# Output projection of a gated multi-branch mixer: seven block products instead of eight

## The chip, the cores and the metric

One Trainium2 chip (trn2), one of its cores. The metric is the device time of one execution in microseconds. All data is float32. A float32 product is made of three TensorE matmuls on operands split into a high part (rounded to fp32r) and a low part (the rest): high x high, high x low, low x high.

## What is computed

One layer, 1024 tokens of 1024 channels. Four branches A, B, C, M come from one input projection; each is projected by its own matrix, weighted by a gate per channel, and summed; the sum goes through the output projection, is added to the scaled input and normalised.

```python
def reference(x, mem, w_in, ...):
    proj = x @ w_in[l]
    ...
    gates = jax.nn.sigmoid(g.reshape(bsz, seq, N_BRANCH, D_MODEL))
    merged = (gates[:, :, 0] * y_a + gates[:, :, 1] * y_b
              + gates[:, :, 2] * y_c + gates[:, :, 3] * y_m)
    out = merged @ w_out[l]
    x = _layer_norm(ALPHA * x + out, ln_g[l], ln_b[l])
```

## The kernel before, in words

The kernel is written engine by engine: each engine has one list of instructions that it works through in order, and waits on semaphores (`s_...`) that other engines raise. So whatever stands behind a waiting instruction in the same list waits too. SyncE (SP) issues all DMAs, also in order.

**Input projection, pairs.** `PAIRS` lists 30 pairs of 256 columns of w_in; pairs 12 to 27 are the gates ("g"). From pair 2 on a pair is one 2x2 block product by seven products (`ORDER` = 1, 5, 6, 2, 7, 3, 4) instead of eight. GpSimd makes the four block sums of the weights (`s_make`, L1595). ScalarE makes the high part (`w_hi_make`, L1130) and GpSimd the low part (`lo_make`, L1571) of each product's weights into a ring of `RING` = 5 slots; the high part of product j waits for product j-5. ScalarE copies products 1, 5, 6 out of PSUM (`copy`, L1138), VectorE sums results 2, 7, 3 (`result`, L1749). Beside it VectorE runs the causal convolution of branch A (`conv_op`, L1785, accumulator in PSUM). The gates go to memory (`gate_scratch`) in 1 MB stores of SP. In pair 24 (`AG0 - 4`) the mean of A's LayerNorm is made: `mean_hi` on ScalarE (L1188) waits on `s_zst`, then its low part on VectorE (L1931), then TensorE's `channel_sum` before the fifth product of the pair.

**Branch projections.** Then come attention and the tiles of P_A, P_B, P_C, P_M (`P_TILES`), each 128 output channels by two halves of 512 tokens: P_C's first two tiles, the eight of P_M (12 matmuls each), then C2 to C7 of P_C (24 each). For a tile s, ScalarE and GpSimd split its weights (`split_w`, L1220, L1624, in two pieces); TensorE makes both halves; VectorE evacuates each with the gate (`p_half`, L2243); GpSimd adds the tile to `merged` (`add_back`, L1700), for P_M VectorE does (L2248). The gate of tile s is loaded by SP (L631) only when tile s-2 has been added, as they share a home. TensorE has four banks here: a half waits until the half four before it was evacuated.

**Output projection.** w_out (1024 x 1024) is loaded in eight blocks of 128 rows at C2 and beside the last tiles (L652, L655). From tile C4 on ScalarE and VectorE split `merged` (L1543, L2256) and w_out (L1550, L2261). TensorE accumulates 16 results (8 tiles of 128 tokens, 2 halves of 512 channels), each over 8 blocks k by three parts: `out_step`, L1074, 384 matmuls, of which the first four results go k by k as `merged` becomes ready. VectorE adds the residual (L2320), makes statistics (L2324, L2327), ScalarE the deviation, and VectorE normalises (L2332, L2337). GpSimd has no part in it.

## Time and profile before

| | us |
|---|---|
| median of 3 runs (lowest, highest) | 1223.47 (1223.08, 1223.71) |
| the profiled execution | 1223.87 |
| its span, first to last instruction | 1222.1 |
| TensorE busy | 1203.0 |
| VectorE, GpSimd, ScalarE busy | 781.5, 693.5, 539.5 |

The span is what the trace covers; the rest of the execution's time, 1.8 us, lies around it. The granted TensorE clock is 0.999 of full speed over the span. In the rows below, PE is TensorE, PEld its weight load, DVE VectorE, ACT ScalarE, POOL GpSimd, SP SyncE. L numbers are lines of the kernel before. "[x <-Y]" at the end of a row says that the engine stood idle for x us ahead of it and what ended the wait. "x2" at the end means that the row merges two instructions, from the start of the first to the end of the last.

### The profile page before, as it was taken

To read this page: it belongs to the slowest core of one execution; us is meant where nothing else is said; L and a number is where in the kernel's file an instruction comes from. 1 tells how busy PE (TensorE), PEld (TensorE's weight loads), DVE (VectorE), ACT (ScalarE), POOL (GpSimd) and SP (SyncE) were. 2 spreads that over 40 slices of the span, in tenths; PEclk is the share of its full clock that TensorE was granted. 3 is DMA by queue.
4 is the path that set the end of the run, shared out by engine and by line. 5 is a ranking of instruction groups with operands and counts; after the bars stand their busy time and mean duration, and the time that the engine had idled before them with its cause. 6 is when DMAs were issued, how large, how long until landed. Compare 5 with 4: busy or idle time off the path is not lost.

```text
span 1222.1 us, 15758 instructions
## 1 busy us (share of the span) xinstructions
PE 1203.0 (98%) x5704; PEld 999.2 (82%) x5704; DVE 781.5 (64%) x1285; ACT 539.5 (44%) x992; POOL 693.5 (57%) x550
## 2 busy tenths in 40 slices
PE   7999999999999999999999999999999999999997
PEld 6888888888888888888888888888888888878886
DVE  4723765677566674438587665666666786876755
ACT  5433434344443443557354565656556444315000
POOL 5677887887777777777226444455533225547000
PEclk9999999999999999999999999999999999999999
DMA  8022131232323423234412111111002533376131
GB/s 278 1 69 69 35 104 35 69 138 101 106 105 103 138 104 104 104 105 148 162 53 56 32 53 52 35 53 46 24 18 92 191 111 116 105 260 241 66 130 69
DMA packets 91277, 118.61 MB, mean 97 GB/s; under 512 B 6072, under 2 KB 72632, under 8 KB 91200
## 3 DMA queue, kind: packets, MB, share of 16 engines
q1 hardware_dynamic: 91200, 117.60, 29.2%
q8 instruction: 46, 0.75, 0.3%
q14 instruction: 31, 0.25, 0.1%
HBM read 92.39 MB, written 25.20 MB: 96 GB/s over the span
## 4 chain that ended last, share of the span: by engine, by line
PE 86%; DVE 7%; ACT 3%; issue 2%; DMA 1%; POOL 1%; DVEq 0%; SPq 0%; ACTq 0%
PE pj L745 11%; PE pj L746 11%; PE pj L747 11%; PE pj L816 5%; PE pj L817 5%; PE pj L818 5%; PE pj L1074 4%; PE pt L746 3%; PE pt L747 3%; PE pt L745 3%; PE po L930 3%; PE pt L917 2%; PE po L1074 2%; PE pt L1074 2%; PE pj L833 2%
## 5 line engine op out<-in xcount | busy, mean ns | idle before, releaser
L1571 POOL TENSOR_TENSOR ring_lo<-w_pair,ring_hi 128x512 fp32r<-128x512 f32 x168 | 232.3, 1385 | 111.3 <-ACT ring_hi L1130 111.1
L1624 POOL TENSOR_TENSOR w_lo<-w_raw,w_hi 128x128 fp32r<-128x128 f32 (+1 forms) x104 | 111.2, 1088 | 161.6 <-ACT w_hi L1220 159.5
L1130 ACT ACTIVATE ring_hi<-w_pair 128x512 fp32r<-128x512 f32 x168 | 105.1, 628 | 160.6 <-PE pj L747 108.6
L1785 DVE SCALAR_TENSOR_TENSOR po<-glu,cwa,po 128x512 f32<-128x512 f32 x232 | 159.4, 747 | 20.6 <-ACT po L1181 20.6
L745 PE MATMUL pj<-t_hi,ring_hi 128*128 128x512 f32 x392 | 152.8, 390 | 0.3 <-DVE slot L1749 0.3
L746 PE MATMUL pj<-t_lo,ring_hi 128*128 128x512 f32 x392 | 152.5, 389 | 0.0
L747 PE MATMUL pj<-t_hi,ring_lo 128*128 128x512 f32 x392 | 152.5, 389 | 0.0
L816 PE MATMUL pj<-xT_hi,w_hi 128*128 128x512 f32 x320 | 126.5, 395 | 0.0
L817 PE MATMUL pj<-xT_lo,w_hi 128*128 128x512 f32 x320 | 125.4, 392 | 0.0
L818 PE MATMUL pj<-xT_hi,w_lo 128*128 128x512 f32 x320 | 125.0, 391 | 0.0
L1664 POOL TENSOR_SCALAR probs<-probs,rinv 128x128 f32<-128x128 f32 (+3 forms) x32 | 57.9, 1810 | 110.8 <-DVE rinv L2103 110.8
L1749 DVE TENSOR_TENSOR slot<-pj,copy_p 128x512 f32<-128x512 f32 x56 | 38.5, 688 | 85.6 <-PE pj L747 85.4
L745 PE MATMUL pj<-xT_hi,ring_hi 128*128 128x512 f32 x224 | 87.1, 389 | 0.0
L746 PE MATMUL pj<-xT_lo,ring_hi 128*128 128x512 f32 x224 | 87.1, 389 | 0.0
L747 PE MATMUL pj<-xT_hi,ring_lo 128*128 128x512 f32 x224 | 87.1, 389 | 0.0
L745 PEld LDWEIGHTS pj<-t_hi,ring_hi 128*128 128x128 f32 x392 | 73.6, 188 | 16.5 <-DVE slot L1749 1.3
L747 PEld LDWEIGHTS pj<-t_hi,ring_lo 128*128 128x128 f32 x392 | 73.6, 188 | 15.3
L746 PEld LDWEIGHTS pj<-t_lo,ring_hi 128*128 128x128 f32 x392 | 73.6, 188 | 15.1
L1595 POOL TENSOR_TENSOR w_pair<-w_pair 128x512 f32<-128x512 f32 x56 | 81.8, 1461 | 6.2
L2115 DVE TENSOR_TENSOR pT_lo<-pt,pT_hi 128x512 fp32r<-128x512 f32 (+2 forms) x96 | 50.4, 553 | 48.4 <-ACT pT_hi L1396 48.4
L1749 DVE TENSOR_TENSOR slot<-pt,copy_p 128x512 f32<-128x512 f32 x28 | 19.4, 692 | 96.6 <-PE pt L747 96.6
L1396 ACT ACTIVATE pT_hi<-pt 128x512 fp32r<-128x512 f32 (+2 forms) x96 | 43.7, 489 | 77.4 <-PE po L930 67.8
(344 smaller groups left out, 2952.1 us busy)
## 6 DMA issues: line engine op xcount, KB each, us to landing
w_pair<-in_w_in SPq DMA_DIRECT2D x28, 1024.0 KB, 5.2
gate_scratch<-slot SPq DMA_DIRECT2D x16, 1024.0 KB, 4.0
gate<-gate_scratch SPq DMA_DIRECT2D x32, 512.0 KB, 3.8
w_raw<-in_w_in SPq DMA_DIRECT2D x20, 512.0 KB, 3.9
z_scratch<-slot SPq DMA_DIRECT2D x8, 512.0 KB, 2.6
bias<-cum_scratch SPq DMA_DIRECT2D x8, 512.0 KB, 3.8
wout_raw<-in_w_out SPq DMA_DIRECT2D x8, 512.0 KB, 5.5
x_tok<-in_x SPq DMA_DIRECT2D x8, 512.0 KB, 4.3
```

Of the source, the lines that this page charges most:

```text
L745: nc.tensor.matmul(dst, w_h, hi, start=k == 0 and p in (1, 2, 5), stop=False, skip_group_check=True)
L746: nc.tensor.matmul(dst, w_h, lo, start=False, stop=False, skip_group_check=True)
L747: mm = nc.tensor.matmul(dst, w_l, hi, start=False, stop=k == KH - 1, skip_group_check=True)
L816: nc.tensor.matmul(pj[:, bank, :], w_hi[:, j % 2, k, :], hi, start=k == 0, stop=False)
L817: nc.tensor.matmul(pj[:, bank, :], w_hi[:, j % 2, k, :], lo, start=False, stop=False)
L818: mm = nc.tensor.matmul(pj[:, bank, :], w_lo[:, j % 2, k, :], hi, start=False, stop=k == nk - 1)
L1074: mm = nc.tensor.matmul(out_bank(n), m, o, start=k == 0 and part == 0, stop=k == KT - 1 and part == 2)
L1130: nc.scalar.activation(ring_hi[:, j % RING, :, :], w_src(u, p), ACT.Copy).then_inc(s_rhi, 1)
L1571: nc.gpsimd.tensor_tensor(ring_lo[:, j % RING, :, :], w_src(u, p), ring_hi[:, j % RING, :, :], ALU.subtract).then_inc(s_rlo, 1)
L1595: nc.gpsimd.tensor_tensor(dst, in0, in1, op).then_inc(s_sadd, 1)
L1624: nc.gpsimd.tensor_tensor(w_lo[:, j % 2, k, :], w_raw[:, j % 2, k, :], w_hi[:, j % 2, k, :], ALU.subtract).then_inc(s_wlo, 1)
L1785: nc.vector.scalar_tensor_tensor(out=acc if n < PAD_A else src, in0=src, scalar=cwa[:, ct, n:n + 1], in1=acc, op0=ALU.mult, op1=ALU.add).t ...
```

## The change

The output projection becomes 2x2 block products too: a unit `u` of four is 256 tokens; it has the blocks a11, a12 (tokens 0 to 127 of the unit, channels 0 to 511 and 512 to 1023), a21, a22 (tokens 128 to 255), and w_out has four blocks of 512 x 512. Seven products a unit, each of 4 k x 3 = 12 matmuls with 512 columns, in the order 1, 5, 6, 2, 7, 3, 4.

- The seven operands from w_out: three are blocks of w_out, four are differences. GpSimd makes these in pairs 13/14, 16/17, 19/20, 22/23 (`block_sum`, four instructions of 512 columns for each of four groups of rows) on rows that SP loads in the pair before, and SP stores them to memory (`out_sums_scratch`, four stores of 1 MB). `mean_hi` now waits for the last of these stores, since they share a home.
- The seven operands, 1 MB each, are loaded at P_M tile 5, at C2, C4, C6, C7 and after, and split: ScalarE `out_block_hi` (2048 columns at once), VectorE `out_block_lo` in four instructions of 512 columns, blocks 0 to 2 behind C3, C4, C5, blocks 3 to 6 behind the last tiles.
- The sums of `merged` blocks are made in place (`merged_sum`): for unit 0 three on VectorE and one on GpSimd, for the others four on GpSimd. High parts of each product's `merged` operand on ScalarE, low parts on GpSimd (`out_lo`), ring of five.
- ScalarE copies products 1, 5, 6 out of PSUM, VectorE adds them to the scaled residual (`with_copy`) and then adds the banks of results 2, 7, 3, 4.
- The last two tiles of P_C run half 0 of both first, then half 1 of both; VectorE adds them to `merged` instead of GpSimd. P_M's odd tiles are added by GpSimd instead of VectorE.
- At the start ScalarE issues the loads of the first weight rows and VectorE makes the first high part of x.

```diff
+    OU = NT // 2
+    OSEQ = [(u, p) for u in range(OU) for p in ORDER]
+    NOQ = len(OSEQ)
+    OSLOT = {up: j for j, up in enumerate(OSEQ)}
+    O_RING = 5
+    OUT_B = {1: 0, 5: 1, 6: 2, 2: 3, 7: 4, 3: 5, 4: 6}
+    LAST_C = S_END - 2
+    def half_no(s, h):
+        return 2 * s + h + 1 if s < LAST_C else 2 * LAST_C + 2 * h + s - LAST_C + 1
+    SUMS_AT = (13, 16, 19, 22)
...
-        if br in (BR_B, BR_C):
+        if br == BR_B or br == BR_C and s < LAST_C or br == BR_M and dt % 2:
             ADD_NO[s] = len(ADD_NO) + 1
-        if br == BR_M:
+        elif br == BR_M:
...
+    ob_at = ((112, 120), (152, 160), (16, 24), (0, 8), (168, 176), (184, 144), (104, 128))
...
+    ob_rows = at_("out_b_rows", [P, 2, D], F32, 48 * KB)
+    o_ring_at = (64, 68, 192, 72, 76)
...
+    o_cp = {p: at_(f"out_copy_p{p}", [P, HALF], F32, o * KB) for p, o in ((1, 80), (5, 82), (6, 84))}
+    o_s1 = at_("out_s1", [P, KH, P], F32, 204 * KB)
...
-                for u in range(2):
-                    sp.dma_start(w_pair[u][:, k, :], pair_src(u, k, k + 1, 0, 2 * P).rearrange("p k c -> p (k c)")
-                                 ).then_inc(s_x11[k], 16)
+                if k:
+                    for u in range(2):
+                        sp.dma_start(w_pair[u][:, k, :], first_w_rows(u, k)).then_inc(s_x11[k], 16)
...
+                if u + 1 in SUMS_AT:
+                    k = SUMS_AT.index(u + 1)
+                    if k == 0:
+                        sp.wait_ge(s_zst, 64)
+                    else:
+                        sp.wait_ge(s_ots, 16 * k)
+                    for n in range(2):
+                        sp.dma_start(ob_rows[:, n, :], w_out[(k + KH * n) * P:(k + KH * n + 1) * P, :]).then_inc(s_wor, 16)
+                if u - 1 in SUMS_AT:
+                    k = SUMS_AT.index(u - 1)
+                    sp.wait_ge(s_ot, 4 * k + 4)
+                    sp.dma_start(t_dram[k, :, :, :], ob_rows[:, :, :].rearrange("p a (b c) -> p (a b) c", b=2)
+                                 ).then_inc(s_ots, 16)
...
+            def load_out_block(n):
+                if n in (0, 3, 5):
+                    kh, nh = {0: (0, 0), 3: (1, 0), 5: (1, 1)}[n]
+                    src = w_out[kh * HALF:(kh + 1) * HALF, nh * HALF:(nh + 1) * HALF].rearrange("(k p) n -> p k n", p=P)
+                else:
+                    src = t_dram[:, :, {1: 0, 4: 1, 6: 2, 2: 3}[n], :].rearrange("k p n -> p k n")
+                sp.dma_start(ob_raw[n][:, :, :], src).then_inc(s_wo[n], 16)
...
+                if s == S_OF[BR_M, 5]:
                     sp.wait_ge(s_tlo, TB_PAIR * CT + 2 * NT)
                     sp.wait_ge(s_pv, PV_PAIR * CT + 2 * NT)
                     sp.wait_ge(s_zpre, CT + MP)
-                    for k in range(2):
-                        sp.dma_start(wout_raw[k][:, :], w_out[k * P:(k + 1) * P, :]).then_inc(s_wo[k], 16)
-                elif s in (S_END - 5, S_END - 4, S_END - 3, S_END - 2, S_END - 1, S_END):
-                    k = s - (S_END - 5) + 2
-                    sp.dma_start(wout_raw[k][:, :], w_out[k * P:(k + 1) * P, :]).then_inc(s_wo[k], 16)
-            sp.wait_ge(s_wlo, 2 * S_END)
+                    load_out_block(0)
+                if s == S_OF[BR_C, 2]:
+                    load_out_block(1)
+                if s == S_OF[BR_C, 4]:
+                    load_out_block(2)
+                if s == S_OF[BR_C, 6]:
+                    sp.wait_ge(s_addm, ADDM_NO[S_OF[BR_M, 4]])
+                    sp.wait_ge(s_add, ADD_NO[S_OF[BR_M, 5]])
+                    load_out_block(3)
+                if s == S_OF[BR_C, 7]:
+                    load_out_block(4)
+                if s == S_END:
+                    load_out_block(5)
+                if s == S_END + 1:
+                    sp.wait_ge(s_pj, 2 * S_OF[BR_M, DT - 1] + 2)
+                    load_out_block(6)
...
+        def out_bank(u, p):
+            return bank((4 + 3 * u + {1: 0, 6: 0, 7: 0, 4: 0, 2: 1, 5: 2, 3: 2}[p]) % 8)
+        def out_src(u, p):
+            if p == 5:
+                return o_s1[:, :, :]
+            k0, n = {1: (0, 0), 6: (0, 0), 2: (KH, 0), 3: (KH, 0), 7: (0, 1), 4: (KH, 1)}[p]
+            return merged[:, k0:k0 + KH, (2 * u + n) * P:(2 * u + n + 1) * P]
...
+        def merged_sum(eng, ops, u, n):
...
+                dst, in0, in1, op = s1, a21, a22, ALU.add
+            elif n == 3:
+                eng.wait_ge(s_osum, O_SUM_NO[u, 1])
+                dst, in0, in1, op = a21, a11, a21, ALU.subtract
+            elif n == 2:
+                eng.wait_ge(s_osum, O_SUM_NO[u, 3])
+                eng.wait_ge(s_orl, OSLOT[u, 1] + 1)
+                dst, in0, in1, op = a11, s1, a11, ALU.subtract
+            else:
+                eng.wait_ge(s_osum, O_SUM_NO[u, 2])
+                eng.wait_ge(s_orl, OSLOT[u, 2] + 1)
+                dst, in0, in1, op = a12, a12, a11, ALU.subtract
...
+            for h in range(2):
+                for s in range(LAST_C, S_END):
+                    pe.wait_ge(s_pjfree, 2 * s + h - 3)
+                    p_steps(s, h, 0, CT, 2 * ((s + 1) % 2) + h)
...
+            def out_product(j):
...
+                elif p == 7:
+                    pe.wait_ge(s_ocp, 3 * u + 3)
+                elif p == 3:
+                    pe.wait_ge(s_ocp, 3 * u + 2)
+                else:
+                    pe.wait_ge(s_yk, 4 * u + 2)
+                pe.wait_ge(s_orl, j + 1)
+                if u == 0:
+                    pe.wait_ge(s_obl, OUT_B[p] + 1)
+                dst = out_bank(u, p)
+                for k in range(KH):
+                    w_h, w_l = o_ring_hi[j % O_RING][:, k, :], o_ring_lo[j % O_RING][:, k, :]
+                    hi, lo = ob_hi[OUT_B[p]][:, k, :], ob_lo[OUT_B[p]][:, k, :]
+                    nc.tensor.matmul(dst, w_h, hi, start=k == 0 and p in (1, 2, 5), stop=False, skip_group_check=True)
+                    nc.tensor.matmul(dst, w_h, lo, start=False, stop=False, skip_group_check=True)
+                    mm = nc.tensor.matmul(dst, w_l, hi, start=False, stop=k == KH - 1, skip_group_check=True)
+                mm.then_inc(s_out_pj, 1)
...
-                act.wait_ge(s_zst, 64)
+                act.wait_ge(s_ots, 16 * KH)
...
+            for u in range(2):
+                act.dma_start(w_pair[u][:, 0, :], first_w_rows(u, 0)).then_inc(s_x11[0], 16)
...
+                nc.scalar.activation(ob_hi[n][:, :, :], ob_raw[n][:, :, :], ACT.Copy, scale=0.5).then_inc(s_obh, 1)
...
+                if S_END - 5 <= s:
+                    out_block_hi(s - (S_END - 5))
+            for j in range(O_RING):
+                out_ring_hi(j)
+            for u in range(OU):
+                for p in ORDER:
+                    if p in (1, 5, 6):
+                        out_copy(u, p)
+                    if u == 0 and p in (1, 5):
+                        out_block_hi(5 + p // 5)
+                    if u and p == 5:
+                        out_std(2 * u - 1)
+                    if OSLOT[u, p] + O_RING < NOQ:
+                        out_ring_hi(OSLOT[u, p] + O_RING)
+                    if p == 4:
+                        out_std(2 * u)
+            out_std(NT - 1)
...
+                if n == 0:
+                    pool.wait_ge(s_wor, 32 * (k + 1))
+                else:
+                    pool.wait_ge(s_ot, 4 * k + n)
+                dst, in0, in1 = ((b11, b12, b11), (b12, b22, b12), (b22, b22, b11), (b21, b21, b22))[n]
+                nc.gpsimd.tensor_tensor(dst, in0, in1, ALU.subtract).then_inc(s_ot, 1)
...
+                    if u in SUMS_AT and p in (3, 4):
+                        block_sum(SUMS_AT.index(u), p - 3)
+                    if u - 1 in SUMS_AT and p in (1, 6):
+                        block_sum(SUMS_AT.index(u - 1), 2 + p // 6)
...
+            def out_lo(j):
+                pool.wait_ge(s_orh, j + 1)
+                nc.gpsimd.tensor_tensor(o_ring_lo[j % O_RING][:, :, :], out_src(*OSEQ[j]), o_ring_hi[j % O_RING][:, :, :],
+                                        ALU.subtract).then_inc(s_orl, 1)
+            for u in range(OU):
+                for p in ORDER:
+                    if p == 1 and u:
+                        merged_sum(pool, nc.gpsimd, u, 1)
+                        merged_sum(pool, nc.gpsimd, u, 3)
+                    out_lo(OSLOT[u, p])
+                    if p == 1 and u:
+                        merged_sum(pool, nc.gpsimd, u, 2)
+                    if p == 2:
+                        merged_sum(pool, nc.gpsimd, u, 4)
...
+            dve.wait_ge(s_x11[0], 48)
+            nc.vector.tensor_copy(xT_hi[:, 0, 0, :], r11[:, 0, :]).then_inc(s_xbh, 1)
...
-                if br == BR_M:
+                if br == BR_M and dt % 2 == 0:
                     dve.wait_ge(s_pjfree, 2 * s + h + 1)
                     dve.wait_ge(s_add, ADD_NO[S_OF[BR_C if dt < 2 else BR_B, dt]])
                     nc.vector.tensor_tensor(merged[:, dt, hs(h)], merged[:, dt, hs(h)], gate, ALU.add).then_inc(s_addm, 1)
+                if s >= LAST_C:
+                    dve.wait_ge(s_pjfree, half_no(s, h))
+                    dve.wait_ge(*added(S_OF[BR_M, dt]))
+                    nc.vector.tensor_tensor(merged[:, dt, hs(h)], merged[:, dt, hs(h)], gate, ALU.add).then_inc(s_addc, 1)
...
+            def out_block_lo(n):
+                dve.wait_ge(s_obh, n + 1)
+                for k in range(KH):
+                    op = nc.vector.scalar_tensor_tensor(out=ob_lo[n][:, k, :], in0=ob_raw[n][:, k, :], scalar=0.5,
+                                                        in1=ob_hi[n][:, k, :], op0=ALU.mult, op1=ALU.subtract)
+                op.then_inc(s_obl, 1)
...
+            for s in range(S_P + IN_M, LAST_C):
                 for h in range(2):
                     p_half(s, h, 2 * ((s + 1) % 2) + h)
-                if s >= S_END - 4:
-                    merged_rest(s - (S_END - 4))
-                    wout_rest(s - (S_END - 4))
-            for k in range(4, KT):
-                wout_rest(k)
-                merged_rest(k)
-            for t in range(NT):
+                if s == S_OF[BR_C, 3]:
+                    out_block_lo(0)
+                if s == S_OF[BR_C, 4]:
+                    out_block_lo(1)
+                if s == S_OF[BR_C, 5]:
+                    out_block_lo(2)
+            for h in range(2):
+                for s in range(LAST_C, S_END):
+                    p_half(s, h, 2 * ((s + 1) % 2) + h)
+                if h == 0:
+                    for n in (1, 3, 2):
+                        merged_sum(dve, nc.vector, 0, n)
+            for n in range(3, 7):
+                out_block_lo(n)
...
+            for u in range(OU):
+                for p in (1, 5, 6):
+                    with_copy(u, p)
+                for p in (2, 7, 3):
+                    out_result(u, p)
+                out_mean(2 * u)
+                if u < OU - 1:
+                    out_norm(2 * u)
+                    out_result(u, 4)
+                    out_mean(2 * u + 1)
+                    out_norm(2 * u + 1)
+            out_norm(NT - 2)
+            out_result(OU - 1, 4)
+            out_mean(NT - 1)
+            out_norm(NT - 1)
```

## Rows read from the trace of the kernel before

**Rows 1.** The profile's page, part 1: busy time, share of the span, instructions

```profile
PE 1203.0 (98%) x5704; PEld 999.2 (82%) x5704; DVE 781.5 (64%) x1285; ACT 539.5 (44%) x992; POOL 693.5 (57%) x550
```

**Rows 2.** Busy us in P_M, P_C, output: PE, PEld, DVE, ACT, POOL; clock, DMA

```profile
1071.40:1094.60 23.20, 22.70 (x98) 17.36 (x96) 18.45 (x27) 4.31 (x16) 11.01 (x18) 1.00 0.76 257
1094.60:1127.30 32.70, 32.70 (x144) 27.06 (x145) 21.52 (x23) 16.79 (x24) 24.04 (x15) 1.00 0.72 255
1127.30:1214.60 87.30, 87.30 (x386) 71.97 (x384) 55.21 (x71) 5.71 (x11) 3.31 (x1) 1.00 0.28 97
```

**Rows 3.** Chain that ended last: start us, us, what

```profile
1149.32 21.76 PE pj L1074 x96
```

**Rows 4.** Timeline, end of P_C: start us, us, engine, line, operation, tiles

```profile
1103.95 2.39 POOL L1700 TENSOR_TENSOR merged<-merged,gate 128x1024 f32<-128x1024 f32 x1 [1.67 <-DVE gate L2243]
...
1128.76 1.21 DVE L2256 SCALAR_TENSOR_TENSOR merged_lo<-merged,merged_hi 128x1024 fp32r<-128x1024 f32 x1
1128.91 3.31 POOL L1700 TENSOR_TENSOR merged<-merged,gate 128x1024 f32<-128x1024 f32 x1 [2.36 <-DVE gate L2243]
1129.89 3.41 DVE L2261 TENSOR_TENSOR wout_lo<-wout_raw,wout_hi 128x1024 fp32r<-128x1024 f32 x1
...
1140.04 1.21 DVE L2261 TENSOR_TENSOR wout_lo<-wout_raw,wout_hi 128x1024 fp32r<-128x1024 f32 x1
```

**Rows 5.** Timeline of POOL and DVE in a pair, at 561 us

```profile
561.06 1.28 POOL L1571 TENSOR_TENSOR ring_lo<-w_pair,ring_hi 128x512 fp32r<-128x512 f32 x1
561.21 2.22 DVE L1956 TENSOR_TENSOR glu<-glu,slot 128x1024 f32<-128x1024 f32 x1
562.49 2.11 POOL L1595 TENSOR_TENSOR w_pair<-s_w,w_pair 128x512 f32<-128x512 f32 x1
```

**Rows 6.** Timeline of DVE and POOL in a gate pair, at 337 us

```profile
337.08 7.32 DVE L1785 SCALAR_TENSOR_TENSOR po<-glu,cwa,po 128x512 f32<-128x512 f32 x11
342.26 1.29 POOL L1571 TENSOR_TENSOR ring_lo<-w_pair,ring_hi 128x512 fp32r<-128x512 f32 x1 [1.91 <-ACT ring_hi L1130]
344.98 1.28 POOL L1571 TENSOR_TENSOR ring_lo<-w_pair,ring_hi 128x512 fp32r<-128x512 f32 x1 [1.43 <-ACT ring_hi L1130]
```

**Rows 7.** End of P_C: POOL, SP, DVE; the page's gate load

```profile
1120.81 5.75 POOL L1700 TENSOR_TENSOR merged<-merged,gate 128x1024 f32<-128x1024 f32 x2
1123.24 0.33 SPq L631 DMA_DIRECT2D gate<-gate_scratch  x1
gate<-gate_scratch SPq DMA_DIRECT2D x32, 512.0 KB, 3.8
1127.56 1.27 DVE L2243 SCALAR_TENSOR_TENSOR gate<-gate,pj 128x512 f32<-128x512 f32 x2
```

**Rows 8.** The mean in pair 24: us to landing of a store; ACT, DVE

```profile
gate_scratch<-slot SPq DMA_DIRECT2D x1, 1024.0 KB, 4.3
...
478.20 1.05 ACT L1188 ACTIVATE ln_mean_hi<-ln_sum 128x1024 fp32r<-128x1024 f32 x1
479.29 1.47 DVE L1931 TENSOR_TENSOR ln_mean_lo<-ln_sum,ln_mean_hi 128x1024 fp32r<-128x1024 f32 x1 [4.45 <-ACT ln_mean_hi L1188]
482.63 0.69 DVE L1749 TENSOR_TENSOR slot<-pj,copy_p 128x512 f32<-128x512 f32 x1 [1.87 <-PE pj L747]
```

**Rows 9.** Timeline of the start: ACT, SP's queue

```profile
0.71 1.28 ACT L1118 ACT_TABLE_LOAD   x1 [0.71 <-PEq L2365]
1.16 0.89 SPq L522 DMA_DIRECT2D w_pair<-in_w_in  x2
5.27 0.63 ACT L1118 ACTIVATE xT_hi<-r 128x512 fp32r<-128x512 f32 x1 [3.27 <-DMA w_pair<-in_w_in]
```

**Rows 10.** PE at the end of P_M

```profile
1094.58 0.50 PE L833 MATMUL pj<-z_hi,w_hi 128*128 128x512 f32 x1 [0.28 <-DVE gate L2243]
```

**Rows 11.** DVE in the tail

```profile
1216.08 0.21 DVE L2327 BATCH_NORM_AGGREGATE mv<-ostats 128x2 f32<-128x12 f32 x1
1216.73 1.27 DVE L2332 SCALAR_TENSOR_TENSOR y_tok<-y_tok,mv,lng_b 128x1024 f32<-128x1024 f32 x1
```

More of the change, by code:

```diff
@@ L670, in _ @@
+            for u in range(1, OU):
+                for q in range(2):
+                    t = 2 * u + q
+                    sp.wait_ge(s_yk, 4 * u - 1 + q)
+                    sp.dma_start(x_tok[:, q, :], x[t * P:(t + 1) * P, :]).then_inc(s_xtk[q], 16)
+                    store_tile(t - 2)
+            store_tile(NT - 2)
             for h in range(2):
@@ L1102, in w_src @@
+            for j in range(NOQ):
+                out_product(j)
         def w_src(u, p):
```

251 lines of the change are left out of this document (132 added, 119 removed).

## Prediction

> **What bounds the kernel now.** I read the table of busy times first: TensorE is busy 98% of the span [rows 1]. So work taken from TensorE is worth its full time, unless an engine that feeds it falls behind. Next I read the stretches that the change touches. From the first P_M tile to the end of P_C, TensorE has hardly a gap, and the output projection is a solid block of 87.3 us [rows 2]; the chain gives 96 of its matmuls 21.76 us, so 0.2267 us each [rows 3]. In the P_C stretch GpSimd is busy 24.0 of 32.7 us and VectorE 21.5; in the output stretch GpSimd does next to nothing (3.3 us) [rows 2]. The change fills exactly this empty engine, so the last view is how VectorE and GpSimd behave when both are busy.
>
> **That view decides the case.** A GpSimd add of 1024 columns takes 2.39 us alone; started at 1128.91, just after a VectorE instruction with two SBUF inputs, it takes 3.31. The VectorE subtraction of 1.21 us alone takes 3.41 when it meets that add [rows 4]. The times fit one pattern to a tenth: the one that comes second stands still until the first has ended (1129.9 + 2.3 = 1132.2 for GpSimd; VectorE then ends at 1133.3), and they take turns, one instruction each. The same at 561: VectorE comes 0.15 us after a GpSimd instruction and takes 2.22 instead of 1.1; the next GpSimd instruction takes 2.11 instead of 1.3 [rows 5]. A VectorE instruction with a PSUM input takes no part: eleven in 7.32 us (0.66 each) run beside a GpSimd instruction that keeps its 1.29 [rows 6]. I count 0.6 us for a 512-column VectorE instruction (two in 1.27 [rows 7]) and 1.25 for a 512-column one of GpSimd.
>
> The Trainium skill says this too (SBUF — State Buffer, "Who interferes with whom"): a VectorE instruction with two SBUF inputs and a GpSimd one that reads SBUF exclude each other for the whole instruction. By that rule the trace agrees, and it speaks against this change; by a shared-bandwidth view (both somewhat slower) the waits below would be about halved. No number here needs the page.
>
> **Part 1, products.** 8 tokens x 2 halves x 8 k x 3 = 384 matmuls become 28 products x 12 = 336. 48 x 0.2267 = **-10.9 us**. A product is 12 x 0.2267 = 2.72 us. The shapes are the same, so the price is.
>
> **Part 2, feeding the first seven products.** Let Z be the end of the last tile's first half (C7, h 0); two more halves follow, so product 1 is due at Z+5.4 and product 4, the last of the seven, at Z+5.4+6x2.72 = Z+21.8. Product 4 waits for VectorE's reading of product 7's bank (s_yk 2). VectorE has in its queue ahead of that:
> - C7 h 0, evacuation and add: 1.3
> - three merged sums, each waiting for the one before: 2.0
> - both second halves, evacuation and add: 2.7
> - the low parts of blocks 3 to 6, four pieces each, 16 x 0.6: 9.6
> - three residual adds: 1.8; result 2 with its statistics and result 7: 1.9
>
> Together 19.3 us. It can't start before the gate of C7 is there. Its load waits for GpSimd's add of C5: the first of two adds begun at 1120.81 ends at about 1123.2, the load is issued at 1123.24 [rows 7], the median from issue to landing is 3.8 [rows 7], and Z in this trace is 1127.3 - 5.4 = 1121.9: so Z+5.2. With no turns the result is there at Z+24.5, a stall of 2.7.
> With turns: 22 to 25 of those instructions have two SBUF inputs, all 16 pieces among them. GpSimd meanwhile has six low parts of the first unit (products 5, 6, 2, 7, 3, 4), its fourth sum, then three sums and three low parts of the second unit: 13 x 1.25 = 16.3. They all read SBUF and interleave one by one with the pieces; a piece costs 1.85 instead of 0.6. Z+24.5+16.3 = Z+40.8, a stall of 19.0 in all, spread over products 2, 7, 3 and 4 (a block takes 7.4 us where a product takes 2.7). From below: only the seven GpSimd instructions that product 4 itself needs (8.8), less 4.2 that fit under VectorE's seven PSUM instructions: stall 7.3. If C7's gate comes 2 us earlier, 17. I take **+18** (2.7 to 20), near the upper end, because rows 4 and 5 show turns each time that both engines are ready. From the second unit on VectorE has 12 us of work in 19 (three residual adds, four results with statistics at 1.2, two tiles' normalising at 2.7 from rows 11), and GpSimd 11 x 1.25 = 13.8 with a lead of five ring slots: no stall, at most 1.
>
> **Part 3, blocks 0 to 2 beside P_C.** Before, a tile's extra VectorE work was two instructions of 1024 columns, each at most one turn. Now it is four pieces after C3, C4, C5: 2.4 us, plus turns with GpSimd's two w_lo pieces (1.4) and its add (2.4 [rows 4]): 6.2, with two evacuations 7.4 per tile of 5.44. VectorE falls back 2 us a tile over three tiles; TensorE has four banks, half of that shows, and the add, the gate load and the next evacuation go later with it. **+3** (0 to 5). The block loads are the bytes of before in other pieces; the first comes earlier, into the P_M stretch, where the DMA engines are busy 76% [rows 2]: 0, up to +2 inside that range.
>
> **Part 4, P_M.** Odd tiles' adds go from VectorE (two of 0.6) to GpSimd (2.4, 11 us busy in 23 [rows 2]). TensorE loses 23.2 - 8 x 2.72 = 1.4 us here; the last wait, for VectorE, is at 1094.58 [rows 10]. The first part of the loss is a late gate, which stays. **-0.3** (-1.3 to +1).
>
> **Part 5, sums of w_out on GpSimd.** Sixteen of 1.3 us, four over two pairs. A pair has idle stretches of 1.91 and 1.43 before its low parts [rows 6], and these run some three products ahead of their use (a low part is released by the product five before it: 5 x 2.72 = 13.6, less 0.6 and 1.3, less the queue). The first sum waits for its rows, behind a gate store, until about 8 us into the pair; GpSimd and, behind it, the low part of product 4 wait, due at 16.3. VectorE's work there has PSUM inputs, no turns. Cost 0 (0 to +1). If the cover goes, each late sum costs 1.3.
>
> **Part 6, the new wait of the mean.** ScalarE's mean_hi now waits for the fourth sums store, issued behind the 1 MB gate store of 473.8. One such store lands after 4.3 us [rows 8], at 478.1; the second goes out 0.4 us behind it and lands between 478.5 (all beside the first) and 482.4 (all after it). I take the middle, 480.6. mean_hi ran at 478.20, so it comes 2.5 later, ends 3.5 after 478.2 at 481.7 and holds up the copy of product 6, which still comes in time; VectorE's low part (1.47) ends at 483.3, and TensorE wants it when product 2 ends, at 482.6 [rows 8]. **+0.9** (0 to +2.5).
>
> **Part 7, start.** The second weight issue goes from SyncE at 1.6 to ScalarE at 1.2, and VectorE makes the first xT_hi, so ScalarE starts on the weights 0.54 us sooner after 5.27 [rows 9]. -0.9 if both count; 0 if ScalarE's table load of 1.28 us stays ahead of the issues. TensorE is full from there on, so it counts. **-0.7**.
>
> **Part 8, tail.** In the last unit tile 6 is normalised before tile 7's last half is read. Result 3 is ready 2.72 before the end: statistics, mean 1.6, two instructions of 1.27 with the reciprocal: free at end+1.65 instead of at once. The deviation now runs beside the centring, -0.4 of the 0.65 between aggregate and centring [rows 11]. **+1.3** (0.8 to 2).
>
> **Sum.** -10.9 + 18 + 3 - 0.3 + 0 + 0.9 - 0.7 + 1.3 = +11.3. The profiled execution took 1223.87 (span 1222.1 and 1.8 around it), 0.4 above the median 1223.47; so 1234.8.
>
> **Rivals.**
> - *Pieces go in a bunch.* VectorE runs the four pieces of a block without letting GpSimd in, since no wait stands between them. For: no row shows four such instructions in a row. Against: at 1129.9 VectorE's next instruction was ready and GpSimd still got its turn [rows 4]. A block then costs 2.4 + 1.25: turns 6 to 8 instead of 13, stall 11 to 12, P_C +1: -10.9+11.5+1+1.2 = +2.8, and up to +6: 1226 to 1230. Slower still, but half.
> - *TensorE stays the bound* (other side, faster). GpSimd has its low parts done before VectorE comes to the blocks, so few turns fall in the stretch, and C7's gate comes at Z+3. The place is the wait of product 4 for s_yk 2; it decides when VectorE's queue with its turns ends before Z+21.8+10, a stall under 10. With stall 3 and P_C 0: -10.9+3+1.2 = -6.7, 1217; with no stall 1214. For: the lead of five slots, and TensorE's solid block in spite of such turns in P_C before. Against: 19.3 us of VectorE's own work from Z+5.2.
> - *The sums starve the ring in the gate pairs* or the mean's wait is long: up to +3 on top of any case.
> - The seven products don't come down to 336 matmuls: hardly, the loops say so.
>
> **Chances.** Turns one by one, my forecast: 0.52, own range 1230 to 1239. Bunched or half: 0.19, 1225 to 1230, with a tenth of it within 0.2%. TensorE bound: 0.27, 1213 to 1221. Rest 0.02. A measurement of this kernel can tell about 0.2% (2.4 us) from no change. Slower by more 0.68, within 0.06, faster 0.26. The range for 8 in 10 has to reach into both: 1215 to 1239.
>
> **What would show it.** In the profile after: 336 output matmuls of 0.227 pitch; TensorE idle before products 2, 7, 3 and 4 of unit 0, released by VectorE's out_b_lo; these pieces at 1.8 us, not 0.6, with GpSimd's out_ring_lo between; GpSimd instructions of 1.9 us there. Units 1 to 3 without gaps. If the pieces show 0.6 each, Part 2 is wrong; if TensorE's gaps in the output stretch sum to under 8 us, the forecast's sign is wrong. Wrong too would be a mean that waits for nothing, or a first matmul as late as before.

## The result, and the profile after

The kernel after takes 1239.29 us (median of 6 runs), the kernel before 1223.59 beside it: a ratio of 1.0125, 95% interval 1.0110 to 1.0139. I had forecast 1234.8, slower by turns of VectorE and GpSimd, range 1215 to 1239. The profiled execution of after took 1237.01 (span 1235.2), 13.1 us of span more than before; the account below is for that execution. The runs of this kernel lie on two levels, near 1237.2 and near 1241.2, and one run of 6877 us stands apart; without it the median is 1237.4. So the median of all six is 0.3 above the top of my range, and that of the five is inside it. What is known of the two levels is told with the experiments.

The page, part 1, of the kernel after (it answers to [rows 1]):

```profile
PE 1197.8 (97%) x5656; PEld 991.6 (80%) x5656; DVE 814.2 (66%) x1309; ACT 556.4 (45%) x1022; POOL 786.1 (64%) x609
```

The busy time of TensorE fell by only 5 us, not by 11, and GpSimd has 93 us more. Busy time in windows of after, for P_M, P_C, the output projection and ten microseconds inside it (columns as in [rows 2]):

```profile
1074.44:1100.83 26.39, 23.05 (x97) 17.53 (x96) 15.23 (x22) 4.30 (x16) 19.55 (x21) 1.00 0.80 256
1100.83:1133.88 33.05, 33.05 (x145) 26.96 (x146) 24.83 (x27) 13.31 (x16) 24.08 (x17) 1.00 0.87 299
1133.88:1226.55 92.67, 81.70 (x337) 65.07 (x335) 85.17 (x93) 28.94 (x49) 66.58 (x40) 0.94 0.27 95
1145.00:1155.00 10.00, 6.77 (x18) 5.04 (x19) 10.00 (x7) 4.28 (x6) 9.25 (x7) 0.66 0.00 0
```

Against [rows 2]: the products are 28 x 12 = 336 matmuls, as forecast (the window counts 337), but they take 92.7 us for 87.3; P_M, where I had forecast a small gain, takes 26.4 for 23.2; P_C, where I had forecast a loss of 3, takes 33.05 for 32.7. In the last row VectorE is busy all of the time, GpSimd nearly so, TensorE two thirds, and its granted clock is 0.66.

Where TensorE stood still in the output projection (timeline: start, us, the instruction; in brackets the idle time before it and what ended it):

```profile
1147.89 0.76 PE L1210 MATMUL pt<-out_b_hi,out_ring_hi 128*128 128x512 f32 x1 [4.35 <-DVE out_b_lo L2443]
1160.30 0.77 PE L1210 MATMUL po<-out_b_hi,out_ring_hi 128*128 128x512 f32 x1 [3.76 <-DVE out_b_lo L2443]
1166.34 0.50 PE L1210 MATMUL pt<-out_b_hi,out_ring_hi 128*128 128x512 f32 x1 [1.70 <-DVE y_tok L2524]
```

These are products 2, 3 and 4 of the first unit; with two small ones (0.72 and 0.34) the gaps sum to 10.9 us. Behind product 4 there is none. The two engines that feed it, VectorE's 16 pieces in one row and three of GpSimd's instructions beside them:

```profile
1140.93 21.64 DVE L2443 SCALAR_TENSOR_TENSOR out_b_lo<-out_b_raw,out_b_hi 128x512 fp32r<-128x512 f32 x16
1149.45 1.73 POOL L799 TENSOR_TENSOR out_s<-merged 128x512 f32<-128x512 f32 x1
1151.25 1.61 POOL L799 TENSOR_TENSOR merged<-merged 128x512 f32<-128x512 f32 x1
1157.90 1.71 POOL L1875 TENSOR_TENSOR out_ring_lo<-merged,out_ring_hi 128x512 fp32r<-128x512 f32 x1
```

**The account.** TensorE's place, after less before: first matmul of L892 (L783 of the kernel before) 18.69 - 19.78 = -1.1; at the mean 485.63 - 482.43 = +3.2; first P_M matmul 1074.44 - 1071.39 = +3.05; first matmul of C2 1100.83 - 1094.58 = +6.25; first output matmul 1133.88 - 1127.39 = +6.5; last matmul's end 1226.49 - 1214.60 = +11.9; end of span +13.1. So the start gave 1.1, the pairs and the mean cost 4.3, P_M 3.2, P_C 0.2, the output 5.4, the tail 1.2 (mean to P_M -0.15).

### The profile page after: what moved, and what is told of

The parts are those of the page before. It is cut to its first block, busy times and chain, and to the rows that moved or that the text cites. A ratio compares the mean times of both kernels' runs of the same rounds, so it can differ in the third digit from the quotient of the medians.

```text
span 1235.2 us, 15869 instructions
## 1 busy us (share of the span) xinstructions
PE 1197.8 (97%) x5656; PEld 991.6 (80%) x5656; DVE 814.2 (66%) x1309; ACT 556.4 (45%) x1022; POOL 786.1 (64%) x609
## 4 chain that ended last, share of the span: by engine, by line
PE 78%; DVE 8%; DMA 4%; ACT 3%; issue 3%; POOL 3%; SPq 0%; DVEq 0%; ACTq 0%; POOLq 0%
PE pj L854 10%; PE pj L856 10%; PE pj L855 10%; PE pj L925 5%; PE pj L926 5%; PE pj L927 5%; PE pt L855 3%; PE pt L856 3%; PE pt L854 3%; PE po L1039 3%; PE pt L1026 3%; DMA gate<-gate_scratch 2%; DVE out_b_lo L2443 2%; PE pj L1009 1%; PE pj L1011 1%
## 5 line engine op out<-in xcount | busy, mean ns | idle before, releaser
L1965 DVE SCALAR_TENSOR_TENSOR po<-glu,cwa,po 128x512 f32<-128x512 f32 x232 | 159.5, 748 | 23.2 <-ACT po L1298 23.2
```

What stands on the lines that cost most here:

```text
L1965: nc.vector.scalar_tensor_tensor(out=acc if n < PAD_A else src, in0=src, scalar=cwa[:, ct, n:n + 1], in1=acc, op0=ALU.mult, op1=ALU.add).t ...
```

## Experiments

In the table each kernel's stretches are between matmuls of its own profile: the start of the mean's first matmul; from the first to the last P_M matmul (M); from there to the first output matmul (C); from there to the last (O). Times in us, medians of 4 or 5 runs (of 6 for after); the ratio is to the kernel before on the same chip.

| kernel | median | ratio, interval | mean at | M | C | O |
|---|---|---|---|---|---|---|
| before | 1223.6 | | 482.4 | 22.5 | 33.5 | 86.8 |
| after | 1239.3 | 1.0110 to 1.0139 | 485.6 | 25.1 | 34.4 | 92.2 |
| e1_whole | 1236.7 | 1.0097 to 1.0127 | 487.8 | 23.8 | 35.9 | 89.2 |
| e2_wait | 1234.9 | 1.0080 to 1.0112 | 485.4 | 25.3 | 34.4 | 88.3 |
| e3_filler | 1241.2 | 1.0121 to 1.0154 | 488.3 | 24.0 | 35.0 | 93.7 |
| e4_nosums | 1233.7 | 1.0069 to 1.0102 | 482.1 | 25.4 | 34.3 | 91.9 |
| e5_adds | 1239.9 | 1.0113 to 1.0162 | 488.3 | 25.3 | 34.9 | 95.0 |
| e6_load | 1240.5 | 1.0125 to 1.0156 | 488.0 | 23.9 | 37.6 | 92.2 |
| e7_shift | 1233.3 | 1.0065 to 1.0099 | 482.0 | 25.3 | 34.4 | 92.3 |
| e8_all | 1232.3 | 1.0059 to 1.0089 | 482.1 | 24.9 | 40.6 | 84.5 |
| e9_both | 1237.2 | 1.0097 to 1.0129 | 488.3 | 22.9 | 35.2 | 92.0 |
| e10_best | 1229.1 | 1.0038 to 1.0070 | 482.9 | 22.1 | 35.5 | 88.2 |
| e11_part | 1230.0 | 1.0041 to 1.0075 | 481.9 | 25.0 | 34.4 | 88.0 |
| e12_clock | 1229.4 | 1.0031 to 1.0059 | 482.6 | 23.0 | 34.6 | 89.6 |

The interval of after overlaps those of e1, e2 (barely), e3, e5, e6 and e9: by their time alone these are not told from it, and what they show is read from stretches of one profile each. The other six are faster than after. Where the output stretch is that of after, O is 91.9 to 92.3 in five kernels and 95.0 in e5, whose profile is of its slowest run (1243.7).

My theory for the output stretch was turns: a VectorE instruction with two SBUF inputs and a GpSimd instruction exclude each other and alternate. The rivals were a proportional slowdown and VectorE's own work.

**GpSimd held back (e2_wait).**

```diff
+                    if p == 1 and u == 1:
+                        pool.wait_ge(s_obl, 7)
                     if p == 1 and u:
                         merged_sum(pool, nc.gpsimd, u, 1)
```

> GpSimd waits until VectorE has made the low parts of all blocks before it starts on the sums of the second unit; nothing else is changed. Theory (turns): of the GpSimd instructions between 1140.9 and 1159.6 the last six belong to the second unit and are not needed before 1168. Without them the last ten pieces have no turn, VectorE ends them some 7 us sooner (1155 for 1162.5), and the kernel takes about 1230 to 1231. Product 1 of the second unit is then fed just in time (three GpSimd instructions, 3.9 us, after 1155). Rival (VectorE's own work sets the stall, not the turns): no gain, and up to 4 us of new waiting for GpSimd, 1237 to 1241.

Measured: 1234.9, less gained than either number of the theory, but its mechanism shows. VectorE's 16 pieces and what GpSimd did, in this kernel's timeline:

```profile
1140.84 15.15 DVE L2445 SCALAR_TENSOR_TENSOR out_b_lo<-out_b_raw,out_b_hi 128x512 fp32r<-128x512 f32 x16
1156.07 2.88 POOL L799 TENSOR_TENSOR out_s<-merged 128x512 f32<-128x512 f32 x1 [6.65 <-DVE out_b_lo L2445]
1159.76 0.50 PE L1210 MATMUL pt<-out_b_hi,out_ring_hi 128*128 128x512 f32 x1 [1.14 <-DVE y_tok L2526]
1181.60 0.50 PE L1210 MATMUL po<-out_b_hi,out_ring_hi 128*128 128x512 f32 x1 [2.35 <-DVE y_tok L2526]
```

The same pieces take 15.15 us for 21.64: six GpSimd instructions fewer beside them, 6.5 / 6 = 1.08 us for each turn. One by one, eleven pieces in after take 1.74 to 1.78 us and five 0.68; here five take 1.75 to 1.78 and eleven 0.68. Product 4 starts 25.6 us after the first output matmul for 32.5. So the turns are real and their work came too early: it belonged to the second unit. But 2.35 us come back in the second unit (last row): GpSimd, now late, meets VectorE's normalising there (four instructions of 1.9 to 2.2 us for 1.28 in after; the three residual adds take 5.2 in both kernels).

**Whole blocks (e1_whole).** One instruction of 2048 columns for the four pieces.

```diff
-                for k in range(KH):
-                    op = nc.vector.scalar_tensor_tensor(out=ob_lo[n][:, k, :], ...
+                nc.vector.scalar_tensor_tensor(out=ob_lo[n][:, :, :], ...
```

> The low part of each block of w_out is one VectorE instruction of 2048 columns instead of four of 512. Theory (each VectorE instruction with two SBUF inputs lets one GpSimd instruction go first): the 16 pieces of blocks 3 to 6 took 21.6 us, of which 16 x 0.6 to 0.68 is their own; as four instructions they have at most four or five turns of 1.3, so some 15 to 16 us; TensorE's stalls in the output stretch fall from 16.4 to about 10, and the time from 1237.2 to about 1231. Rival (the two engines slow each other in proportion to their bytes): the same 21 us, 1237. Second rival: GpSimd now stands still 2.4 us at a time, its own low parts come late and TensorE waits for these instead, 1234 to 1237.

Measured: 1236.7; O falls by 3.0, half of what I expected, and C grows by 1.5. From its timeline:

```profile
1142.63 13.23 DVE L2442 SCALAR_TENSOR_TENSOR out_b_lo<-out_b_raw,out_b_hi 128x2048 fp32r<-128x2048 f32 x4
1147.11 9.89 POOL L1875 TENSOR_TENSOR out_ring_lo<-merged,out_ring_hi 128x512 fp32r<-128x512 f32 x3
1155.79 5.14 DVE L2509 SCALAR_TENSOR_TENSOR x_tok<-x_tok,out_copy_p 128x512 f32<-128x512 f32 x3
```

The blocks take 13.2 for 21.6, which rules out a slowdown in proportion to bytes: the bytes are the same. But GpSimd now pays 3.3 us for each low part that takes 1.25 alone, and its turns of the second unit fall on the three residual adds, 5.1 us for 1.9. The turns were moved, not removed; the second rival of this run is half right. The Trainium skill (SBUF — State Buffer, "Who interferes with whom") has the lock held for the whole instruction; by that rule a long instruction hurts the other engine in proportion to its length, and this trace agrees (a low part of 1.25 us alone takes 3.3 beside 2048 columns, 1.7 beside 512).

**Does the clock cost anything? (e3_filler)**

```diff
                 if u == 0:
+                    for _ in range({2: 17, 3: 14}.get(p, 0)):
+                        nc.tensor.matmul(bank(7), ob_hi[1][:, 0, 0:P], ob_hi[1][:, 0, :], ...)
                     pe.wait_ge(s_obl, OUT_B[p] + 1)
```

> TensorE gets 17 matmuls of its own before the wait of product 2 of the first unit and 14 before that of product 3, into a bank that nobody reads: 3.85 and 3.2 us at 0.2267 each, inside the waits of 4.35 and 3.76 that the trace shows there. Nothing that others wait for comes later. Theory: the granted clock fell to 0.66 to 0.85 in this stretch because TensorE stood still, and that costs 5.5 of the 16.4 us lost; with the filler the clock stays at 1.0 and the time falls to 1232 to 1234. Rival: the clock falls there for another reason, or the slow matmuls only fill time in which VectorE is the bound anyway: 1237, with longer waits in place of the slow matmuls.

Measured: 1241.2, O 93.7: the rival. The clock of 1145 to 1155 was 1.00 instead of 0.66, and product 4 started 32.4 us after the first output matmul, as in after (32.5). Its start is set by VectorE, so slow matmuls ahead of it fill a wait and cost nothing. Drops came at other places: behind a wait of 2.7 us before product 7, and behind the wait of 2.6 us before product 4, where some ten matmuls ran at a pitch of 0.43; the latter nothing hides.

**The pairs (e4_nosums, e7_shift).** e4 leaves out every `block_sum`, and SyncE's store waits for the rows instead, so that blocks 1, 2, 4 and 6 hold plain rows. Of e7:

```diff
-                    if u in SUMS_AT and p in (3, 4):
-                        block_sum(SUMS_AT.index(u), p - 3)
-                    if u - 1 in SUMS_AT and p in (1, 6):
-                        block_sum(SUMS_AT.index(u - 1), 2 + p // 6)
+                    if u - 1 in SUMS_AT and p in (6, 7, 3, 4):
+                        block_sum(SUMS_AT.index(u - 1), (6, 7, 3, 4).index(p))
```

> GpSimd makes no block sums of w_out in the gates' pairs; the rows are loaded and stored as before, so blocks 1, 2, 4 and 6 are plain rows and the output is not the reference's. Theory (GpSimd stood 4.4 us for the rows, then ran behind; its late sums of w_pair held up ScalarE, which held up the convolution's first copy, behind which VectorE read a bank 2.5 us late): the 2.7 us lost before the mean go, the mean's own wait of 0.9 stays, 1234 to 1234.5. Rival a (the loads and stores of 6 MB disturb the pairs): 1237. Rival b (the late mean comes from the same backlog of GpSimd): 1233.

> The four block sums of a group of rows are made one pair later, in one pair, after the low parts of products 6, 7, 3 and 4, where GpSimd had idle stretches of 1.3, 1.9 and 1.4 us before the change, and the rows have long landed. Theory (standing 4.4 us for the rows and sums ahead of s_w is what set GpSimd back): the wait of 2.5 us at 414 goes and the time falls to 1233.5 to 1234.5; the last store goes out up to 4 us later, so the mean may wait 1 to 3 instead of 0.9, in which case 1235 to 1236. Rival (GpSimd has no room for 5.2 us in a pair of 19, wherever they stand): 1237 or more.

Measured: 1233.7 and 1233.3; the mean starts at 482.1 and 482.0 for 485.6. The loads and stores are there in both, so they are not the cause, and GpSimd has room for the sums, so that isn't either: it is where they stand (e7 takes away both GpSimd's standing for the rows and their places ahead of s_make; which of the two counts isn't told apart). Kernel after, timelines of GpSimd, ScalarE, VectorE, TensorE:

```profile
384.91 1.29 POOL L1755 TENSOR_TENSOR out_b_rows<-out_b_rows 128x512 f32<-128x512 f32 x1 [4.44 <-DMA out_b_rows<-in_w_out]
401.80 0.63 ACT L1247 ACTIVATE ring_hi<-w_pair 128x512 fp32r<-128x512 f32 x1 [3.60 <-POOL w_pair L1745]
404.14 1.46 DVE L1965 SCALAR_TENSOR_TENSOR po<-glu,cwa,po 128x512 f32<-128x512 f32 x2 [8.97 <-ACT po L1298]
413.64 0.50 PE L854 MATMUL pj<-t_hi,ring_hi 128*128 128x512 f32 x1 [2.53 <-DVE slot L1929]
```

GpSimd stands 4.4 us for the rows and never catches up in that pair. Its late s_make holds ScalarE 3.6 us in order; behind that waits ScalarE's first step of a convolution, so VectorE, idle 9 us, begins it 1.4 us later than in the kernel before (402.73), and the sum behind it takes 2.27 us for 1.63; behind these stands the reading of a bank, which TensorE needs. In the kernel before the same bank was read at 410.85, here at 412.91, though this kernel had started 1.1 us earlier. GpSimd stands 4.4 us in each of the four groups; only in this one does TensorE come to wait.

The levels: from the first matmul of L892 to the mean's first matmul the kernel before takes 462.65 us, the six kernels without the wait at 414 (e4, e7, e8, e10, e11, e12) 463.8 each, after and e2 466.9 and 467.0. In the profiles of e1, e3, e5, e6 and e9, which keep this wait, the seven or so matmuls behind it run at a pitch of 0.43 instead of 0.23, and it is 468.4 to 468.6. So the mean's own wait costs 1.15 us, this one short wait 3.15 and, in some executions, 1.5 more. What is left of the differences under "mean at" arose before: the matmuls of L892 begin at 18.04 to 19.83 us in the 13 kernels, whose code is the same up to there. The runs of e4, e7, e8, e11 and e12 lie within 0.9 to 2.5 us, but e10, also without the wait, has one run at 1232.8 above three at 1228.6 to 1229.4. So where the 4 us between the two levels come from stays open but for these 1.5.

**P_M (e5_adds, e6_load, e9_both).** e5 takes the odd tiles' adds back to VectorE (the first two hunks; a wait of SyncE follows them), e6 loads block 0 with C2 instead of M5 (the last hunk), e9 does both:

```diff
-        if br == BR_B or br == BR_C and s < LAST_C or br == BR_M and dt % 2:
+        if br == BR_B or br == BR_C and s < LAST_C:
-                if br == BR_M and dt % 2 == 0:
+                if br == BR_M:
...
-                if s == S_OF[BR_M, 5]:
+                if s == S_OF[BR_C, 2]:
```

> The adds of the odd P_M tiles are made by VectorE again, two of 512 columns each, as before the change. P_M lasts 26.4 us in the kernel after against 23.2 before, where I had forecast a gain of 0.3. Theory: a GpSimd add of 2.4 us stands ahead of the w_lo pieces, the weight slot comes free later, its load is issued later (1087.34) and TensorE waits; with the adds back P_M takes 23.2 to 24 and the kernel 1234 to 1235. Rival (the 1 MB load of block 0, issued at 1082.96, holds up the weights behind it): no change, 1237, and the next run shows the gain.

> The load of block 0 is issued with tile C2 instead of M5, right ahead of that of block 1. Theory (GpSimd's adds cost the 3.2 us of P_M): no gain there, at most 0.5; 1236.5 to 1238, since the low part of block 0 has 6 us to spare. Rival (that load costs them): P_M takes 23.2 to 24, 1234 to 1235.

> Both edits of the two kernels before in P_M: the odd adds on VectorE and block 0 loaded with C2. Alone, neither brought P_M back (25.3 and 23.9 us for 25.05, with TensorE waiting for late gates in the one and for w_lo in the other). Theory: two causes, each enough by itself to make a wait; with both gone P_M takes 23.2 to 23.6, as before the change. P_C then has 2 MB at once at its start and takes 36 to 37.5 as it did with block 0 at C2 (37.4) for 34.2, so the whole stays at 1237 to 1241. Rival (something else in P_M, as the gates' homes, costs it): P_M still 24.5 or more.

Measured: M is 25.3, 23.9 and 22.9 for 25.1; before it was 22.5. Kernels whose P_M is that of after spread over 23.8 to 25.4, so neither edit alone is told from nothing, and my first theory (the adds alone) falls. The spread goes with the time at which P_M is reached: 23.8 and 24.0 in e1 and e3, which are late at the mean, 24.9 to 25.4 in the six others. The two edits together are below the kernels of their own kind in e9 (late, 22.9), and so are e10 and e12 (22.1, 23.0), which load block 0 with M7. In after:

```profile
1083.63 2.40 POOL L1864 TENSOR_TENSOR merged<-merged,gate 128x1024 f32<-128x1024 f32 x1 [1.70 <-DVE gate L2425]
1087.04 0.47 PE L942 MATMUL pj<-zm_hi,w_hi 128*128 128x512 f32 x1 [1.01 <-POOL w_lo L1788]
1087.34 0.38 SPq L532 DMA_DIRECT2D w_raw<-in_p_m  x1
1091.76 0.51 ACT L1337 ACTIVATE w_hi<-w_raw 128x128 fp32r<-128x128 f32 x2 [5.12 <-DMA w_raw<-in_p_m]
```

The add stands ahead of the w_lo pieces, for which TensorE waits 1.01 us at 1087.04 and, behind the add of 1097.41, 0.95 ahead of C2. The weights' slot is free late too and the load goes out at 1087.34; it then needs over 4 us among the others, and TensorE waits 1.12 us for the gate at 1093.87. In e5 the two waits for w_lo are gone, but weights whose load goes out 1.5 us behind block 0, with its 1 MB ahead of them, come late (ScalarE waits 5.39 us), and TensorE waits 0.89, 1.30 and 0.36 us for gates. In e6 and e9 the block was moved into P_C, and C grew by 3.2 and 0.8. So the P_M loss needed both the adds and the load, as far as three profiles against eight can say; why e6's P_C lost more than e9's stays open.

**Putting it together (e8_all, e10_best, e11_part, e12_clock).**

e8 is e1, e2 and e7 with one edit more:

```diff
                 if s == S_OF[BR_C, 5]:
                     out_block_lo(2)
+                    out_block_lo(3)
...
-            for n in range(3, 7):
+            for n in range(4, 7):
                 out_block_lo(n)
```

> One instruction for a block's low part (e1), GpSimd's second unit after the blocks (e2), the sums one pair later (e7), and the low part of block 3 made right after that of block 2, while VectorE waits for the last gate. Theory: the turns were most of the stall, so with four blocks fewer and longer, three of them left after the last halves and GpSimd held back, VectorE ends them at 1150 to 1151 and product 4 starts some 3 us late instead of 16: 1237.2 - 2.7 (pairs) - 11 to 13 = 1221.5 to 1224. Rival (VectorE is late anyway through its waits for copies and through the turns of the second and third unit, as the 2.35 us wait in the third unit of e2 shows): 1226 to 1230.

Measured: 1232.3. O is 84.5, below the 86.8 of before and the shortest of all; but C grew from 34.4 to 40.6 and took it all. From its timeline:

```profile
1120.86 5.51 POOL L1786 TENSOR_TENSOR w_lo<-w_raw,w_hi 128x128 fp32r<-128x128 f32 x2
1126.42 0.80 PE L942 MATMUL pj<-z_hi,w_hi 128*128 128x512 f32 x1 [1.99 <-POOL w_lo L1786]
1133.06 0.69 DVE L2425 SCALAR_TENSOR_TENSOR gate<-gate,pj 128x512 f32<-128x512 f32 x1 [6.14 <-DMA gate<-gate_scratch]
```

Two w_lo pieces that take 1.4 us alone each wait for a VectorE instruction of 2048 columns; TensorE waits for them (1.18 and 1.99 us), twelve matmuls behind the second wait run at a pitch of 0.43 (2.4 us), the add is late, and the last gate's load with it. Beside P_C the cut into pieces is right: in the kernel after, no matmul of P_C waited behind the first of C2.

e10 keeps the pieces of blocks 0 to 2, halves those of 3 to 6 (two instructions of 1024), lets GpSimd wait for `s_pre` 3 instead of `s_obl` 7, shifts the sums, and has e5's edit and block 0 with M7; e11 is e10 without the last two.

```diff
+                step = 1 if n < 3 else 2
+                for k in range(0, KH, step):
+                    r = slice(k, k + step)
...
+                    if p == 1 and u == 1:
+                        pool.wait_ge(s_pre, 3)
```

> What the kernels so far point to: sums one pair later; GpSimd starts on the second unit when VectorE has made the three residual adds of the first (in the kernel that made whole blocks these adds took turns, 5.1 us for 1.9); the low parts of blocks 3 to 6 in two instructions of 1024 columns, those of 0 to 2 in four; odd adds of P_M on VectorE; block 0 loaded with M7. Theory: output stretch from 92.6 to 86 to 87, P_M 23.5 to 24.5, P_C 34 to 35, pairs as in the kernel with the shifted sums: 1225 to 1227.5. Rival (VectorE's queue of two normalisings in the second unit is the next bound, a wait of 2.4 us there grows to what the first unit gave back): 1229 to 1231.

> As the kernel before, with P_M as in the change (odd adds on GpSimd, block 0 with M5). Theory: 1 to 1.5 us more than that kernel, all of it between the first P_M tile and the output stretch, which is the same 86 to 87: 1226.5 to 1229. Rival: the same or less than that kernel, because the loads of block 0 two tiles later are given back in P_C.

Measured: 1229.1 and 1230.0, the rival of e10 in its size; the two can't be told apart. M fell to 22.1, but TensorE then waits 2.35 us ahead of C2: M and C together are 57.6 for 59.4 in e11. O fell only to 88.2. Product 4 starts 25.2 us after the first output matmul, no better than in e2, and then:

```profile
1154.87 0.80 PE L1210 MATMUL pt<-out_b_hi,out_ring_hi 128*128 128x512 f32 x1 [2.93 <-DVE y_tok L2526]
1176.20 0.67 DVE L2526 TENSOR_TENSOR y_tok<-x_tok,po 128x512 f32<-128x512 f32 x1
```

and, in windows of the same kernel (columns as in [rows 2], the clock third from the end):

```profile
1155.00:1165.00 10.00, 10.00 (x32) 7.97 (x33) 6.42 (x9) 3.95 (x6) 9.71 (x7) 0.70 0.17 54
```

Fourteen matmuls at 0.43 instead of 0.23 follow the last wait: 2.8 us that nothing hides, unlike those ahead of product 4 in after. e12 is e10 with 8, 5 and 11 filler matmuls before products 2, 7 and 4.

> The best kernel so far (sums shifted, GpSimd held back, halves of blocks, odd adds on VectorE, block 0 with M7) with matmuls of its own for TensorE, into a bank that nobody reads, ahead of the waits of products 2 (8), 7 (5) and 4 (11) of the first unit: 1.8, 1.1 and 2.5 us at 0.2267, a little less than the waits of 2.05, 1.47 and 2.93 there. In that kernel the first 14 matmuls after the last wait came at a pitch of 0.43 instead of 0.23, 2.8 us lost behind the last thing that TensorE waits for. Theory: the granted clock falls when TensorE stands still; kept busy, it stays at 1.0 and the 2.8 us go, 1226 to 1227 for 1229.1. Rival (as in the first kernel with such matmuls: the drop only moves to a later place, or the fillers run slow and push product 4): 1229 to 1231.

Measured: 1229.4 (1.0045 for 1.0054: the same). Its timeline:

```profile
1154.36 0.50 PE L1214 MATMUL pt<-out_b_hi,out_ring_hi 128*128 128x512 f32 x1 [0.42 <-DVE y_tok L2530]
1176.41 0.50 PE L1214 MATMUL po<-out_b_hi,out_ring_hi 128*128 128x512 f32 x1 [2.37 <-DVE y_tok L2530]
1177.97 0.63 PE L1216 MATMUL po<-out_b_hi,out_ring_lo 128*128 128x512 f32 x1
```

```profile
1155.00:1165.00 10.00, 9.90 (x44) 7.92 (x43) 7.38 (x10) 3.87 (x7) 9.71 (x8) 1.00 0.21 74
```

The fillers did keep the clock, as its window shows (44 matmuls for 32): behind product 4 the pitch is 0.23. The 2.8 us came back as the next wait, product 4 of the second unit for VectorE's reading of result 7, and a new drop behind it (granted clock 0.83 from 1176 to 1186). In e10 that reading came at 1176.20 and TensorE reached the product at 1176.92, just late enough not to wait. So once the first unit is mended VectorE's queue is the bound in the second as well, and no version here beats the kernel before; the best, e10 and e12, which can't be told apart, are 0.5% slower than it.

## Why the prediction was right, and where not

- **Products, -10.9**: right. From product 4 of the first unit to the end are 22 products in 1226.49 - 1166.34 = 60.15 us, 2.73 each.
- **The first seven products, +18**: the mechanism right, the size 1.6 too high. The output stretch is 92.7 and 28 products are 76.2, so 16.5 were lost: 10.9 of gaps, most of the rest slow matmuls between them (18 at about 0.43). With Z = 1133.88 - 5.44 = 1128.4, VectorE has C7's gate at Z+4.8 (forecast Z+5.2), ends the pieces at Z+34.1 (Z+37.1) and TensorE starts product 4 at Z+37.9 (Z+40.8). The mis-sized term is the price of the turns, 13 x 1.25 = 16.3: the count was right (13 GpSimd instructions from 1136.15 to 1159.61), but eleven of them fall on pieces and cost 1.08 each, one costs a merged sum 1.1 (1.80 for 0.69), and the last at most 0.4; 13.4 in all. TensorE waited before 2, 3 and 4 and hardly before 7; I had named all four. The eleven pieces that met a turn took the forecast 1.8, the other five 0.68, so the average is 1.35. The bunch rival is out.
- **No stall from the second unit on**: right for this kernel. It held because GpSimd had done its second unit early, in the stretch where it hurt. e2 and e12 show the wait of 2.4 us that appears when it hasn't (1.0 us in e11; in e10 TensorE came 0.7 us too late to wait). My sum of VectorE's 12 us in 19 left out the turns in the normalising and in the residual adds (5.2 us for 1.9).
- **P_C, +3**: wrong, it cost 0.2. The pieces did take turns (4.7 to 5.8 us a tile where I had 6.2), but VectorE had entered the stretch with gaps of its own and the four banks took the rest. e1 and e8 show how near the edge is.
- **P_M, -0.3**: wrong, +3.2. The step that failed was "odd tiles' adds go to GpSimd, 11 us busy in 23": I priced the work and not what stands behind it, the w_lo pieces, the weights' slot and its load; and I took block 0's load, in a stretch whose DMA engines were busy 76%, as 0 (up to 2, under P_C). P_M and P_C together I had at 2.7 and they are 3.4, so the sum came out nearly right by two errors.
- **Sums of w_out, 0 (0 to +1)**: wrong, +3.15 (from L892 to the mean 466.95 in after, 463.8 in e4 and e7). I saw that the first sum waits for its rows and that GpSimd stands for it, but checked only the low part due next. The loss took the chain of four engines shown above, and "each late sum costs 1.3" has no counterpart in it.
- **The mean, +0.9**: right; TensorE waited 0.94 for ln_mean_lo, 1.15 us in its place, and ScalarE waited 2.10 for the store, where I had 2.5. It lands 6.1 us after its issue, between the bounds of [rows 8]. In e4 and e7 it is the same.
- **Start, -0.7**: -1.1, though w_pair landed no sooner; the first matmul began 0.25 earlier and ran less behind its operands. The other twelve kernels, with the same start, show from +0.05 to -1.7, so the one number says little.
- **Tail, +1.3**: 1235.2 - 1226.49 = 8.7 for 7.5, +1.2.

The sum was 11.3 and the profiled execution shows 13.1. The errors that mattered were 3.1 too little in the sums and 3.5 in P_M, two places where GpSimd got work "beside" others, against 2.8 too much in P_C and 1.6 in the output. The large term, the turns, was foreseen; that the sum comes within 2 us is luck, as these errors of some 6.6 and 4.4 us nearly cancel. The median of all runs is 2.3 above the profiled execution, since three of the six (two on the upper level and the one of 6877 us) lie above 1241, which I hadn't foreseen.

## What to carry to other kernels

Before giving an idle engine more work, list what stands behind each new instruction in its queue and follow that through every in-order queue to the bound engine: here 4.4 us of standing passed through GpSimd, ScalarE and VectorE and cost TensorE 3.15. Where VectorE and GpSimd exclude each other, hold back the work that is not yet due, and cut the instruction to the other engine's need: short beside a queue that must move (P_C), long where nothing waits for the other. Removing one wait of a critical engine is worth only the distance to the next one, so look for that before the edit.

## What the runs showed of the hardware that I had not expected

- After TensorE had waited 2.5 us at 414, its next matmuls ran at a pitch of 0.43 instead of 0.23 in five of seven profiles and at full speed in two. The five came to this place 0.7 us or more later than the two (L892 at 19.36 to 19.83 for 18.40 and 18.69); whether that decides it isn't shown. In the output stretch the granted clock was 0.66 to 0.83 over ten microseconds, which is a mixture of 2.4 and 1.2 GHz, but after the wait of 2.35 us in e2 no matmul was slow. With matmuls of its own in the waits (e12) it stayed at 1.00 from 1155 to 1165.
- Whether such a drop costs anything depends on what comes next: nothing in the output stretch of after, where a later wait was set by VectorE, and 2.8 us in e10, where none followed.
- VectorE and GpSimd took turns one instruction each, with short and with long instructions of VectorE: a GpSimd instruction of 1.25 us cost 3.3 beside 2048-column instructions and 1.7 beside 512-column ones.
